# Opening of a two-block transformer kernel: order of tiles, banks and first transfers

## The reference

```python
f1 = swiglu(rms_norm(x, ffn1_pre_g[l]), ffn1_w_gate[l], ffn1_w_up[l], ffn1_w_down[l])
# swiglu: (silu(h @ w_gate) * (h @ w_up)) @ w_down
```

## Time and profile before

| | |
|---|---|
| Median of 3 runs | 992.85 us |
| The profiled execution's own time | 992.94 us |
| Its span, first to last instruction | 991.1 us |
| PE busy | 985.8 us (99%) |
| PE weight loads busy | 835.6 us (84%) |
| DVE busy | 711.4 us (72%) |
| ACT busy | 486.5 us (49%) |
| POOL busy | 213.2 us (22%) |
| Transfers | 178.53 MB, mean 180 GB/s |

### The profile page before, as it was taken

The page is one execution under the profiler, slowest core; times in us unless marked ns, Lnnn a source line. Parts: engine busy times, 40 slices in busy tenths (PEclk is TensorE's granted clock), DMA queues, the critical chain, the costliest instruction groups (busy, mean ns, idle before and its releaser), DMA issues.

```text
span 991.1 us, 14543 instructions
## 1 busy us (share of the span) xinstructions
PE 985.8 (99%) x5302; PEld 835.6 (84%) x5302; DVE 711.4 (72%) x849; ACT 486.5 (49%) x621; POOL 213.2 (22%) x215
## 2 busy tenths in 40 slices
PE   8999999999999999999999999999999999999998
PEld 6888888888888888888888888888888888888887
DVE  5766767775788767676777998677876767666664
ACT  6534343664665533434545444465555445334342
POOL 3313232014100222222112600060000012223230
PEclk9999999999999999999999999999999999999999
DMA  9665656745325555565745625544536356555561
GB/s 311 227 211 171 208 173 199 268 128 192 127 87 170 203 179 204 176 203 178 240 156 177 204 95 196 190 145 148 170 118 222 129 187 233 170 179 201 179 206 44
DMA packets 121065, 178.53 MB, mean 180 GB/s; under 512 B 5808, under 2 KB 82160, under 8 KB 120896
## 3 DMA queue, kind: packets, MB, share of 16 engines
q1 hardware_dynamic: 120048, 174.86, 52.8%
q0 software_dynamic: 576, 1.39, 0.5%
q10 hardware_dynamic: 400, 1.73, 0.5%
HBM read 176.88 MB, written 2.64 MB: 181 GB/s over the span
## 4 chain that ended last, share of the span: by engine, by line
PE 99%; DMA 0%; ACT 0%; SPq 0%; DVE 0%; issue 0%
PE acc L662 11%; PE acc L666 10%; PE acc L665 10%; PE tp L861 10%; PE gu L861 10%; PE gu L866 5%; PE tp L866 5%; PE tp L662 4%; PE tp L666 4%; PE tp L665 4%; PE gu L662 3%; PE gu L666 3%; PE gu L665 3%; PE acc L1141 2%; PE acc L1144 1%; PE acc L1170 1%
## 5 line engine op out<-in xcount | busy, mean ns | idle before, releaser
L2001 DVE TENSOR_TENSOR wlo<-raw,whi 128x2048 fp32r<-128x2048 f32 x140 | 325.5, 2330 | 153.8 <-ACT whi L1361 152.2
L1361 ACT ACTIVATE whi<-raw 128x2048 fp32r<-128x2048 f32 x150 | 285.8, 1908 | 70.2 <-PE acc L666 22.9
L861 PE MATMUL tp<-act_in,whi 128*128 128x512 f32 x432 | 102.9, 390 | 0.0
L861 PE MATMUL gu<-act_in,whi 128*128 128x512 f32 x432 | 102.6, 390 | 0.0
L1898 POOL TENSOR_TENSOR tmp<-tmp 128x256 f32<-128x256 f32 x54 | 39.8, 737 | 276.2 <-DVE tmp L2122 276.2
L1900 POOL TENSOR_TENSOR sil<-sil,tmp 128x256 f32<-128x256 f32 x54 | 88.7, 1642 | 33.7 <-ACT sil L1432 33.7
L861 PEld LDWEIGHTS gu<-act_in,whi 128*128 128x128 f32 x432 | 80.9, 188 | 16.6
L662 PE MATMUL acc<-whi,hT_hi 128*128 128x512 f32 x240 | 94.0, 392 | 0.0
L665 PE MATMUL acc<-wlo,hT_hi 128*128 128x512 f32 x240 | 93.7, 390 | 0.0
L666 PE MATMUL acc<-whi,hT_lo 128*128 128x512 f32 x240 | 93.4, 389 | 0.0
L861 PEld LDWEIGHTS tp<-act_in,whi 128*128 128x128 f32 x432 | 79.8, 188 | 15.7
(11 more groups left out here) (379 smaller groups left out, 1845.0 us busy)
## 6 DMA issues: line engine op xcount, KB each, us to landing
raw<-in_w_in SPq DMA_DIRECT2D x96, 512.0 KB, 4.5
raw<-in_down SPq DMA_DIRECT2D x66, 512.0 KB, 4.1
raw<-in_gate SPq DMA_DIRECT2D x64, 512.0 KB, 4.3
raw<-in_up SPq DMA_DIRECT2D x64, 512.0 KB, 4.7
raw<-in_w_out SPq DMA_DIRECT2D x16, 512.0 KB, 4.7
raw<-in_w_branch_hg SPq DMA_DIRECT2D x8, 512.0 KB, 4.3
raw<-in_w_branch_attn SPq DMA_DIRECT2D x8, 512.0 KB, 4.7
post<-in_post_gains SPq DMA_DIRECT2D x3, 512.0 KB, 6.0
```

Of the source, the lines that this page charges most:

```text
L861: pe.matmul(banks[:, a, :], w_hi[:, i, a * P:(a + 1) * P], both, start=i == 0, stop=False)
L1361: act.activation(split_weights(k)[0], raw[:, k % RING, :], ACT.Copy).then_inc(hi_ready, 1)
L2001: dve.tensor_tensor(w_lo, raw[:, k % RING, :], w_hi.bitcast(F32), ALU.subtract).then_inc(lo_ready, 1)
```

## The change

Tiles of part 1 get a bank each: tiles 0 and 1 the two banks of `tp`, tiles 2 and 3 the banks of `acc` that tiles 0 and 1 of part 0 had. For those PE first waits until DVE has finished rest(0,1) (`tile_lo` at 2). Each tile is signalled, and waited for, by itself. The orders on ACT and DVE change. `hot` and `rel` become one array `bias_parts` (32 partitions by 264 values), brought by one transfer. ACT's queue then issues the first up half, which goes out of SP's list; the later entries of SP's list move up by one.

```diff
-        hot = sb("hot", [REL_BUCKETS, S])
+        bias_parts = sb("bias_parts", [REL_BUCKETS, S + 8])
+        hot, rel = bias_parts[:, 0:S], bias_parts[:, S:S + 8]
...
         def first_bank(i, a):
-            return tp[:, a // 2, a % 2 * P:(a % 2 + 1) * P] if i else acc[:, a // 2, a % 2, 0:P]
+            return tp[:, a, 0:P] if i and a < 2 else acc[:, (a - 2 * i) // 2, a % 2, 0:P]
...
             def half_piece(j, a):
-                for w, m in enumerate((wg_d[0], wu_d[0])):
+                for w, m in enumerate((wg_d[0], wu_d[0])[:2 if j or a else 1]):
...
                     for a in range(4):
+                        if i and a == 2:
+                            pe.wait_ge(tile_lo, 2)
                         mm = pe.transpose(first_bank(i, a), from_x(t, 4 * h + a), idn)
-                        if a < 3 and (i == 0 or a == 1):
+                        if a < 3:
                             mm.then_inc(tile_turned, 1)
...
-                pe.wait_ge(bias_parts_in, 16 * 2)
+                pe.wait_ge(bias_parts_in, 16)
...
                 for a in range(2):
-                    pe.wait_ge(tile_lo, 4 + a)
+                    pe.wait_ge(tile_lo, 3 + a)
                     product(0, 1, a)
...
             def first_turned(i, *tiles):
-                    if a == 3 or i and a == 2:
+                    if a == 3:
                         act.wait_ge(turn_full, i + 1)
                     else:
-                        act.wait_ge(tile_turned, 4 if i else a + 1)
+                        act.wait_ge(tile_turned, 3 * i + a + 1)
...
-            for dst, src in ((hot[:, :], hot_d), (rel[:, :], rel_d)):
-                act.dma_start(dst, src).then_inc(bias_parts_in, 16)
+            act.dma_start(bias_parts[:, :], bias_parts_d).then_inc(bias_parts_in, 16)
+            act.dma_start(raw[:, 0, :].rearrange("p (k n) -> p k n", k=4)[:, 0:2, FC:2 * FC],
+                          wu_d[0].rearrange("(k p) n -> p k n", p=P)[:, 0:2, 0:FC]).then_inc(part_in[0], 16)
             act.wait_ge(pool_step, 1)
             load_table(0, ACT.Silu)
-            first_turned(0, 0, 1, 2)
+            first_turned(0, 0)
             first_hi(0, 0, 1)
+            first_turned(0, 1)
+            first_hi(0, 1, 1)
+            first_turned(0, 2)
+            row_from_bank()
+            first_turned(1, 0, 1)
             first_turned(0, 3)
-            first_hi(0, 1, 1)
-            row_from_bank()
-            first_turned(1, 0, 1, 2, 3)
+            first_turned(1, 2, 3)
             first_hi(0, 2, 1)
...
-            first_rest(0, 0, 1, 2)
+            first_rest(0, 0)
             first_lo(0, 0, 1)
-            first_rest(0, 3)
+            first_rest(0, 1)
             first_lo(0, 1, 1)
-            first_rest(1, 0, 1, 2, 3)
+            first_rest(1, 0, 1)
+            first_rest(0, 2, 3)
+            first_rest(1, 2, 3)
             first_lo(0, 2, 1)
```

More of the change, by code:

```diff
@@ L127, in build @@
 def build(nc, x_d, wg_d, wu_d, wd_d, win_d, wout_d, win2_d, whg_d, wat_d, wout2_d,
-          fixed_d, rows_d, post_d, rel_d, level_d, hot_d, out_d, row_d, skew_d):
+          fixed_d, rows_d, post_d, bias_parts_d, level_d, out_d, row_d, skew_d):
     with ExitStack() as ctx:
@@ L177, in build @@
         rows = sb("rows", [P, R_END])
-        rel = sb("rel", [REL_BUCKETS, 8])
         mhalf = sb("mhalf", [P, 32])
@@ L769, in first_block @@
                 warm_up(3)
-                pe.wait_ge(bias_parts_in, 16 * 2)
-                pe.matmul(gu[0:8, 1, 0:S], rel[:, :], hot[:, :], start=True, stop=True).then_inc(row_product, 1)
+                pe.wait_ge(bias_parts_in, 16)
+                pe.matmul(gu[0:8, 1, 0:S], rel, hot, start=True, stop=True).then_inc(row_product, 1)
                 for a in range(2):
@@ L1660, in first_turned @@
                 for a in tiles:
-                    if a == 3 or i and a == 2:
+                    if a == 3:
                         act.wait_ge(turn_full, i + 1)
                     else:
-                        act.wait_ge(tile_turned, 4 if i else a + 1)
+                        act.wait_ge(tile_turned, 3 * i + a + 1)
                     ins = act.activation(first_place(i, a)[0], first_bank(i, a), ACT.Copy, scale=first_gain(i, a))
[L1666 to L1669, removed]
+                    ins.then_inc(act_hi_ready if a == 3 else tile_hi, 1)
             def row_from_bank():
@@ L2444, in first_rest @@
                 for a in tiles:
-                    if a == 3 or i and a == 2:
+                    if a == 3:
                         dve.wait_ge(act_hi_ready, i + 1)
                     else:
-                        dve.wait_ge(tile_hi, 4 if i else a + 1)
+                        dve.wait_ge(tile_hi, 3 * i + a + 1)
                     hi, rest = first_place(i, a)
@@ L2845 @@
     arrays["post_gains"] = np.concatenate([of(n, 1, D) for n in ("ffn1_post_g", "mix_post_g", "ffn2_post_g")], axis=0)
-    arrays["rel_table"] = of("rel_bias_table_2", REL_BUCKETS, 8)
+    arrays["bias_parts"] = np.concatenate([hot_np, of("rel_bias_table_2", REL_BUCKETS, 8)], axis=1)
     arrays["level_masks"] = lv.reshape(P, -1)
-    arrays["one_hot"] = hot_np
     nc = bacc.Bacc("TRN2", target_bir_lowering=False, num_devices=1)
@@ L2856 @@
           [d[f"down{f}"] for f in range(3)], d["w_in"], d["w_out"], d["w_in_2"], d["w_branch_hg_2"],
-          d["w_branch_attn_2"], d["w_out_2"], d["fixed"], d["packed_rows"], d["post_gains"], d["rel_table"],
-          d["level_masks"], d["one_hot"], out, row, skew)
+          d["w_branch_attn_2"], d["w_out_2"], d["fixed"], d["packed_rows"], d["post_gains"], d["bias_parts"],
+          d["level_masks"], out, row, skew)
     r = run_bass_kernel_spmd(nc, [{"in_" + n: a for n, a in arrays.items()}], core_ids=[0])
```

## The result

The changed kernel takes 994.94 us (median of 18 executions, 993.65 to 996.73), against 992.84 for the kernel before in the same measurement. The ratio is 1.0019, interval 1.0012 to 1.0026: slower by about 1.9 us (2.1 by the medians). I had forecast 992.93, with 992.3 to 993.6 around it, so the time lies outside. The 18 executions fall into groups by their mean granted clock: eight at 1.000 (993.65 to 994.42, median 993.96), nine at 0.998 (994.89 to 995.80, median 995.16) and one at 0.996 (996.73). All listed executions of the kernel before but one lie within 992.43 and 993.19 (the one at 995.97). There are therefore two losses: about 1.1 us in every execution, and another 1.2 in half of them (2.8 in the slowest). The profiled execution belongs to the first group: own time 993.65, span 991.9, against 992.94 and 991.1 in the table of before.

The account below looks back on a forecast made before the run. PE was taken as the bound, without gaps after 9.77 us, so only the start of its unbroken run could move. Tile order -0.37 plus up half +0.45 gave +0.08: median 992.93, range 992.3 to 993.6.

Parts of the forecast that it names:

- the price of the first up half: Opening: up, now competing with x part (1,0), lands later and shifts the first product; +0.45 us, bounds -0.25 to +0.7.
- My second rival: Opening: SP's queue goes first, up lands at 7.15 or up to 0.4 later; +0.33 to +0.73, about 993.35; chance 0.27.
- one for one between the queues: Opening transfers: both queues move packets equally, so only 32 rows of x precede up's last; +0.18.
- The row of `rel`: Opening transfers: its landing at 6.18 despite few rows taken to show that what is issued together lands together.
- The tile order: PE's stop before product(0,1,0): part 1's tiles signalled singly start it at 9.40 rather than 9.77; -0.37 us, bounds 0 to 0.44.
- The margin at lo(1,2,2): DVE's split before its first reader at 16.74: cover of 0.27 becomes 0.05; loss up to 0.1 us possible, zero taken.
- The new wait in turn(1): PE waiting for rest(0,1): costs nothing if DVE keeps time, 0.1 if the pairing of load and matmul breaks.
- the joined array: Bias tables on ACT's queue: one issue instead of two, landing covered by PE's warm-ups; zero.
- The clock, given 0.03: PE idle from about 6.95 to 7.7 makes its rate fall back; +1.5 us, some 994.5; chance 0.03.

Follow-up runs that it names:

- the second profile of before: The unchanged kernel before, profiled once more; own time 992.68 us, constants and first up half landing earlier than in the first profile.
- The swap of the queues: Changed kernel with x part (1,0) third on ACT's queue and the first up half third on SP's; 993.94 us (1.0015).
- the seven profiles counted above: All profiles with the first up half third on SP's queue; hi(0,0) starts at 5.88 to 6.03 in five, 6.46 and 6.52 in two.
- the first experiment: Changed kernel with the first up half back on SP's queue as third issue, all else kept; 992.61 us (0.9999).
- the second experiment: Kernel before with only the joined bias array and the first up half on ACT's queue, old tile order; 995.29 us (1.0025).

## Why the prediction was wrong

**The step that failed is the price of the first up half, "+0.45 us"**. Measured from the profile that I had, hi(0,0) moved from 6.46 to 7.30, +0.84; from the second profile of before, 5.97 to 7.30, +1.33. My second rival, "Up lands behind x part (1,0)", is what happened: it put the landing at 7.15 or up to 0.4 later, and it was 7.3. I had given it 0.27 against 0.42. The first product came 0.77 after hi(0,0), as forecast, so the whole miss is in the landing.

What led me off was one for one between the queues, counted from the start. The packets shown with the result agree with one for one from 4.4 to 6.4 (259 and 249). But by 4.4 SP's queue had moved 384 packets and ACT's 193. I had let 416 rows of ACT's queue run beside 384 of SP's, as if the two began level, so that only 32 rows of x got ahead of up's end. Up really began when SP's queue was nearly through its first two transfers (416 packets, where it stops when x part (1,0) is held back). So up had all of x part (1,0) beside it, and part of the gate half behind that. What the counts don't explain is up's end: few of its packets are left at 6.4, and it lands at 7.28. The row of `rel`, which I took as a sign that what is issued together lands together, was 0.7 us late by itself. The swap of the queues shows the company of x as the cause and that no queue has precedence for the landing, and holding SP's list back gives the whole price. The Trainium skill's rule of turns by whole packets ("DMA: Bandwidth & Descriptors", "Queues, rings and completion order") fits the landing of 7.3, but the swap fits plain sharing as well, with up last on either queue, so no run here proves it. The same page's rule that spreading over issuing engines gains no bandwidth ("Rules for kernel authors") the runs bear out: gate half (0,1), issued 0.5 us earlier in the changed kernel, landed at 7.87, against 7.89 and 7.69 in the two profiles of the kernel before.

**The term was also measured from an unlucky baseline.** Landings in the kernel before vary by 0.5 to 0.7 us from one execution to the next (4.8 and 4.3 for up, 4.5 and 3.8 for `rel`), and by the seven profiles counted above the early landing is the common one. With the first product at 7.06 rather than 7.23 there was more to lose.

**The sum, put right.** From the second profile of before: first product +1.01 (7.06 to 8.07; less than the transfer's 1.33, since PE was busy until about 7.06 with warm-ups at its slow pace and the bias product); to product(0,1,0) -0.19 (2.38 to 2.19); lo(1,2,2) +0.06, as product(0,1,0) to L861 or L863 goes from 10.59 to 10.65. That is +0.88, the shift of that line (20.03 to 20.91), and own times differ by 0.97. From the profile that I had, the same three are +0.84, -0.35 and +0.01, in all +0.50 where the forecast had +0.08; own times differ by 0.71, and the other 0.2 lie in the unchanged work after L861.

**The tile order was right.** -0.37 forecast; where the first product waits for the split, first product to product(0,1,0) goes from 2.54 to 2.19, -0.35, and the stop from 0.44 to 0.08 (0.07 forecast). Where PE itself is late, as in the second profile of before and in the first experiment, it goes from 2.38 to 2.02, -0.36. With a late transfer in both it is 0.36 or 0.51, by the way of comparing (changed kernel against the second experiment, executions at 1.000; only three of these). Little of it reaches the median when the transfer is early: 992.61 against 992.69. In some executions PE is late itself, as shown there; whether this accounts for the rest is open, since the stretch from L861 to the last matmul, with the same work in it, also varies between 967.73 and 968.03 us from one profile to another.

**The margin at lo(1,2,2)** was named as the narrowest place, with up to 0.1 lost. It closed, and cost 0.01 to 0.10: product(0,1,0) to L861 takes 10.59 to 10.64 with the old order (three profiles), and to L863 10.65 and 10.66 in the two profiles read above, 10.65 to 10.69 in three others. That term holds.

**The new wait in turn(1) and the joined array** cost nothing, as forecast.

**The clock, given 0.03, decided half of the executions.** I forecast a stand of 0.75 us and set 0.76 before 5.13 against it. The stand became 1.73 in the profiled execution, and nine of 18 executions paid about 1.2 us, a further one 2.8 (1.5 forecast for the case). Two wrongs met: the stand was longer through the transfer, and the 0.76 was a poor witness, as it lay before the faster rate had set in or just as it did: the warm-ups ahead of it start 0.43 apart, and later matmuls of the same size 0.23. The two warm-up experiments move this group at will: none with eight warm-ups, three to six of eleven without any. The Trainium skill ("TensorE: Matmul & The Clock Gate", "HAM oscillation — how this bites in real kernels") warns that waits for transfers can throw PE back to half its clock; the trace agrees, 0.51 behind a stand of 1.90. The waits in that section's example are longer, some 3 to 5 us; here 1.90 and 1.09 were enough in executions whose traces show the fall. Together the two cases, up late and clock fallen, would have given 992.85 + 0.33 to 0.73 + 1.5, some 994.7 to 995.1, and the second group is at 995.16. I had treated them as rivals to each other, though the first brings on the second.

## What to carry to other kernels

Where the DMA engines are full, a transfer is late by what is issued beside it, on either queue: count what each queue has moved by the time the transfer really starts, keep what the first product waits for ahead of what is needed a microsecond later, and put a transfer on a second queue only if what moves up in the first can come later. Ask of every added wait on PE whether it brings the clock down, and fill it with idle matmuls before anything else; rivals that cause one another belong in one case, with one price. And profile the kernel before twice where the argument hangs on a landing time.

## What the runs showed of the hardware

The landing of a first transfer of 256 KB varied by 0.5 us and that of one of 1 KB by 0.7 us between executions of one kernel, with issue times alike to 0.01. PE's faster rate sets in at different times in the same opening (four transposes at about 4.5 us took 0.66 in one profile and 1.11 or 1.12 in others). The clock came down in ten of 18 executions of the kernel whose profile shows a stand of PE of 1.73 us early on, in eight of eleven with one of 1.90, in three of eleven with one of 1.09, in none of eleven with one of 0.90 (eight warm-ups), and in one of eleven with one of 0.79 (up ahead of the bias tables); but also in five of eleven of a kernel whose profiled execution stood for 0.62 only (the queues swapped). Each of these stands is read from one profiled execution, and the others' may differ. In the kernel without second warm-ups the clock fell between 7 and 8 us, with PE at work again since 6.65. In the first microseconds the clock column reads 1.00 while 512-column matmuls start 0.43 apart.
